# The last gate/up chunk of each expert as two loads of 1 MB with 8 KB pieces

## The reference

```python
logits = jnp.dot(x, w_router).astype(f32) + b_router.astype(f32)
top_val, top_idx = lax.top_k(logits, TOP_K)
gates = jax.nn.softmax(top_val, axis=-1)
...
def expert_block(args):
    xb, e = args
    gu = jnp.dot(xb, w_gate_up[e]) + b_gate_up[e]
    g = jnp.minimum(gu[:, :D_FF], SWIGLU_LIMIT)
    up = jnp.clip(gu[:, D_FF:], -SWIGLU_LIMIT, SWIGLU_LIMIT)
    hdn = (up + 1.0) * (g * jax.nn.sigmoid(SWIGLU_ALPHA * g))
    return jnp.dot(hdn, w_down[e]) + b_down[e]
```

## Time and profile before

| | before |
|---|---|
| median of three runs | 1271.97 us |
| the profiled execution | 1272.08 us |
| its span, first to last instruction | 1270.4 us |
| mean granted TensorE clock | 0.989 |
| PE busy | 1230.2 us (97%) |
| DVE / POOL / ACT busy | 465.4 / 242.9 / 174.7 us |
| read from HBM | 437.39 MB |
| DMA packets | 69352, of them 44744 under 8 KB |

### The profile page before, as it was taken

How to read it: one execution, slowest core, us unless ns; L and a number is a source line. 1 busy time by engine, 2 the same in 40 slices (tenths; PEclk the granted TensorE clock), 3 DMA queues, 4 the chain that set the end, 5 groups by cost and what they waited for, 6 DMA issues and landing times.

```text
span 1270.4 us, 21490 instructions
## 1 busy us (share of the span) xinstructions
PE 1230.2 (97%) x7739; PEld 553.7 (44%) x7740; DVE 465.4 (37%) x915; ACT 174.7 (14%) x311; POOL 242.9 (19%) x438
## 2 busy tenths in 40 slices
PE   7999999999899999999999999999999999999997
PEld 4666666668533333333334333333333333333332
DVE  6667767333522332222223222222223322222224
ACT  4651105214400000000000000000000000000002
POOL 2067760000211111111111211111111121111100
PEclk9989999999799999999999999999999999999999
DMA  8323232459699999999999999999999999999994
GB/s 227 99 68 100 87 105 75 155 184 385 231 393 428 428 427 428 429 427 429 429 428 429 429 429 428 428 428 429 429 428 429 429 428 429 428 429 427 428 429 187
DMA packets 69352, 440.31 MB, mean 347 GB/s; under 512 B 13024, under 2 KB 42376, under 8 KB 44744
## 3 DMA queue, kind: packets, MB, share of 16 engines
q1 hardware_dynamic: 66952, 438.72, 83.9%
q10 hardware_dynamic: 2368, 1.15, 0.3%
HBM read 437.39 MB, written 1.87 MB: 346 GB/s over the span
## 4 chain that ended last, share of the span: by engine, by line
PE 68%; DMA 25%; DVE 4%; issue 1%; SPq 0%; ACT 0%; DVEq 0%; POOL 0%; ACTq 0%; POOLq 0%
DMA big<-in_w_gate_up_dram 25%; PE psum L916 23%; PE psum L519 14%; PE psum L955 13%; PE psum L897 5%; PE psum L883 4%; PE psum L497 3%; PE psum L797 3%; PE psum L531 1%; PE psum L628 1%; PE psum L925 1%; PE psum L942 1%; DMA cst<-in_consts_dram 0%; PE psum L639 0%; DVE acc L1836 0%
## 5 line engine op out<-in xcount | busy, mean ns | idle before, releaser
L916 PE MATMUL psum<-big,m 128*64 128x512 f32 x2048 | 473.6, 599 | 13.0 <-DMA big<-in_w_gate_up_dram 10.0
L1797 DVE TENSOR_TENSOR acc<-acc,psum 128x512 f32<-128x512 f32 (+1 forms) x192 | 123.1, 681 | 583.4 <-PE psum L897 583.4
L916 PEld LDWEIGHTS psum<-big,m 128*64 128x64 f32 x2048 | 137.4, 137 | 320.0 <-issue 257.2
L955 PE MATMUL psum<-big,m 128*64 128x512 f32 x1024 | 226.8, 595 | 0.0
L519 PE MATMUL psum<-big,m 128*128 128x320 f32 x576 | 167.6, 447 | 3.2 <-issue 1.9
L1353 POOL COPY m<-uT 96x64 bf16 x32 | 7.5, 235 | 662.1 <-PE psum L942 661.7
L519 PEld LDWEIGHTS psum<-big,m 128*128 128x128 f32 x576 | 109.7, 195 | 55.1 <-issue 15.7
L955 PEld LDWEIGHTS psum<-big,m 128*64 128x64 f32 x1024 | 70.7, 137 | 134.1 <-issue 127.9
L897 PE MATMUL psum<-m 64*128 64x512 f32 (+1 forms) x384 | 106.7, 632 | 0.0
L1239 ACT ACTIVATE m<-m 128x512 f32<-128x512 f32 x32 | 20.2, 630 | 561.1 <-DVE m L1810 561.1
L1362 POOL TENSOR_SCALAR m<-cst,m 128x128 f32<-128x128 f32 x96 | 75.0, 792 | 7.7 <-POOL m L1357 7.7
(11 more groups left out here) (283 smaller groups left out, 851.2 us busy)
## 6 DMA issues: line engine op xcount, KB each, us to landing
big<-in_w_gate_up_dram SPq DMA_DIRECT2D x128, 2048.0 KB, 29.4
big<-in_w_down_dram SPq DMA_DIRECT2D x64, 2048.0 KB, 31.1
m<-in_w_in_dram SPq DMA_DIRECT2D x18, 1024.0 KB, 5.2
m<-in_w_s_glu_dram SPq DMA_DIRECT2D x8, 512.0 KB, 4.3
m<-in_w_out_dram SPq DMA_DIRECT2D x3, 1024.0 KB, 5.7
acc<-in_x_prompt_dram SPq DMA_DIRECT2D x4, 512.0 KB, 5.4
m<-in_w_ml_out_dram SPq DMA_DIRECT2D x2, 1024.0 KB, 5.0
big<-in_w_out_dram SPq DMA_DIRECT2D x1, 1024.0 KB, 7.6
```

Of the source, the lines that this page charges most:

```text
L916: mm = pe.matmul(psum[SLOT * hf:SLOT * hf + SLOT, GB + gu, :], xeT[:, GU_CHUNKS * k + c, :], big[:, base:base + 512], start=(c + k == 0), ...
L955: mm = pe.matmul(psum[SLOT * hf:SLOT * hf + SLOT, DB, :], hT[:, m, c, :], big[:, base:base + 512], start=False, stop=(c == DN_CHUNKS - 1 a ...
L1797: v.tensor_tensor(x, x, psum[0:n, CB + hf, :], ALU.add).then_inc(S("added"), 1)
```

## The change

`expert_chunk` issues the last gate/up chunk (`c` = 3) as two loads: the first takes the `k` = 0 half (one row of 8 KB for each partition, every other row of the matrix) and raises `w_landed` of the slot as before; the second takes the `k` = 1 half and raises a new semaphore, `w_half0` for even `r` and `w_half1` for odd `r`. PE waits for the new semaphore before the first `k` = 1 matmul of that chunk. Both destinations are the same places of the ring as before, the other five chunks are as before, and so is the count that frees slots.

```diff
@@ expert_chunk
             if c < GU_CHUNKS:
                 row = 2 * c * P
                 src = a["w_gate_up"][0, bass.ds(e, 1), row:row + 2 * P, :].rearrange("a (p k) n -> p (a k n)", k=2)
+                if c == GU_CHUNKS - 1:
+                    eng.dma_start(dst[:, 0:CHUNK], src[:, 0:CHUNK]).then_inc(S(f"w_landed{k}"), 16)
+                    eng.dma_start(dst[:, CHUNK:WIDE], src[:, CHUNK:WIDE]).then_inc(S(f"w_half{r % 2}"), 16)
+                    return
             else:
@@ expert, on PE
                     for c in range(GU_CHUNKS):
                         pe.wait_ge(S(f"w_landed{slot(r, c)}"), 16 * loads(turn_, r, c))
                         for k in range(2):
+                            if c == GU_CHUNKS - 1 and k == 1:
+                                pe.wait_ge(S(f"w_half{r % 2}"), 32 * turn_ + 16 * (r // 2 + 1))
                             for gu in range(2):
```

## The result

| | before | changed |
|---|---|---|
| median (lowest to highest) of 15 runs | 1271.84 us (1269.35 to 1273.61) | 1275.4 us (1272.98 to 1278.21) |
| profiled execution / its span | 1272.08 / 1270.4 us | 1275.22 / 1273.4 us |
| DMA packets | 69352 | 73969 |
| instruction blocks fetched (queue q8) | 21, 0.34 MB | 30, 0.49 MB |
| instructions of PE in the built program | 1842 | 1854 |

The change makes the kernel slower by 0.32% (ratio 1.0032, 95% interval 1.0024 to 1.0040); the medians are 3.6 us apart. 1273.8 was forecast, with a range of 1271.2 to 1277.0. The ratios in this document leave out every execution that took over 1.5% longer than the fastest of its kernel: two of e2's six and two of e10's seven.

The account below looks back on a forecast made before the run. The prediction took the unbroken DMA stream of weights (the belt), plus the last expert's work, to bound the kernel. Packets +2.0 us and earlier last start -0.24 us gave +1.8 us: 1273.8 us, range 1271.2 to 1277.0.

Parts of the forecast that it names:

- The belt bounds, and only what lengthens it counts: Weight stream, unbroken from about 380 us: added belt time is paid in full, PE time saved before the end is worth nothing.
- Term 1: Belt: the split adds 9 packets per engine and expert at 7.5 ns, 68 ns; 30 experts pay, +2.0 us.
- b: Price of a byte on one engine, 0.0368 ns, solved from 16 KB gate/up loads and 1 KB-piece w_in loads.
- the skipped-read rival: Split loads: reading every other 8 KB is slower, 0.48 us more per chunk, +14 us, 1286; chance 6%.
- Term 2: Last expert's fourth chunk: its first half lands earlier, so PE starts 0.24 us sooner, -0.24 us.
- Term 3: Other belt-paced experts: the same 0.24 us is given back waiting at the next expert's first chunk; worth nothing.
- it would be repaid out of the ring's stock: Stage paced by PE: a passed wait costing PE a few ns is made up from loaded chunks; no net cost.
- The first wait of PE about one expert earlier: Sign of being right: PE first waits for a load about one expert earlier, as the stock falls faster.
- faster, 7%: Whole kernel faster by over 0.2%: nearly all from the fourth-chunk wait being on the path, -3.0 us, rival's chance 8%.
- slower by over 0.2%: Whole kernel over 2.5 us slower: 35%, from dearer packets (24), load-end cost (5) and skipped reads (6).
- within 0.2%: Whole kernel within 2.5 us, not told from no change: 58%, including 13 for free extra packets.

Follow-up runs that it names:

- e2: Kernel before plus only a second, never-waiting wait before the fourth gate/up chunk's k = 1 matmuls, loads unchanged; median 1283.99 us, ratio 1.0062.
- e10: The change itself, unaltered, run again on the same chip as e11; 1277.49 us, ratio 1.0039 against the kernel before.
- e3: Kernel before with all four gate/up chunks as two 1 MB loads of 8 KB pieces, awaited once per chunk; 1285.86 us, ratio 1.0104.
- e5: Kernel before with all four gate/up chunks as single 2 MB loads, but of 8 KB pieces; 1280.79 us, ratio 1.0067.
- e11: The kernel of e8 run again, on the same chip as e10; 1273.78 us, ratio 1.0018 against the kernel before.
- e8: The change with two of PE's three signals per expert that nobody waits for left out; 1274.05 us, ratio 1.0021 against the kernel before.
- e7: Kernel before with gate/up chunks loaded in pairs, 4 MB loads of 32 KB pieces, and two unused signals per expert left out; 1274.00 us, ratio 1.0019.

## Why the prediction was right and where it was not

*The belt bounds, and only what lengthens it counts:* right where PE does not pause. The pace late in the loop is 29.44 us for the 29.43 forecast, at a DMA share of 1.01.

*Term 1, 68 ns per expert from nine packets of 7.5 ns:* right in size, and that by two errors that nearly cancel. Measured 74 ns ((1231.82 - 996.32) / 8 = 29.44 against 29.364), from eight pieces at 9.2 to 9.7 ns, a quarter dearer than forecast, and an end packet of about 1 ns where 7.5 was put. Over 30 experts that is +2.2 us, for 2.0. One row was misread on the way: the five full slices aren't within one load. With the slices beside them they add up to 2.1 MB, so they run over two w_in loads back to back; the sum stands as it is, since their seam belongs to the price. And that w_in pieces "fit the same b" is no argument against the skipped-read rival, since b was worked out from them; what removes it is e3 against e5.

*Term 2, -0.24 us at the end:* right (0.30 in the profile). *Term 3,* the same start given back at the next expert: right, 0.55 us of waiting for the 0.4 forecast.

*What failed* is the sentence in term 3 that if a wait cost PE anything, "it would be repaid out of the ring's stock". It priced the added instructions by the time they take, a few ns, and never asked what the code's length does where the loop jumps back. The pause is 6.7 us of PE. One of them, early, is mostly repaid from the stock, as the sentence says, but not wholly: places come free late, the loads issued from 470 to 490 us have only about 10 to 11 us from issue to landing where e11's have 18, so fewer are queued, and from 450 to 520 us the belt moves 29.4 MB where e8 and e11 move 29.9, about 1.2 us less. e8 and e11 put the change without pauses at +0.21% and +0.18%, close to the +0.14% forecast, and the change itself stands at +0.32% and +0.39%. That the pauses cost something is shown by e10 beside e11; how much is known only roughly, about 2 us there, and the single profiled executions say less (the last expert begins at 1231.82 us in the change's, at 1230.31 and 1231.59 in e8's and e11's). With seven pauses the stock is gone and the kernel takes 1303 us.

*Luck.* The result lies in the range, but the sum has no term for the pauses. The range held them because it had room for dearer packets and for the spread of the runs, and because none of the fifteen executions took as long as many pauses make it (the longest 1278.21 us, a little outside). Two of e10's seven, the same kernel, lie far above 1277.0.

*"The first wait of PE about one expert earlier"* was wrong for the same reason: it comes at 976.67 us (0.18 us, then 0.55 at 996.32) and not before 876.10, since PE was 6.7 us behind. Without the pause it comes true: e11's first wait is at 848.71, one expert earlier, and e8's at 827.92.

*The chances:* faster, 7%, is excluded by the interval. The result lies in the part given 35%, slower by over 0.2%; the forecast of a change within 0.2% holds for the change without the pauses only as far as its intervals (0.12 to 0.30% and 0.09 to 0.27%) reach.

## What to carry to other kernels

Where one queue is busy without a gap, a split that lets an engine start sooner buys only the last start, here 0.3 us, and pays for every piece in every round, here 9.4 ns each. Price added instructions in a written-out loop also by the loop's length: look in the timeline at the first instruction after each jump back, and in the instruction queue at the blocks fetched; eight instructions decided here between no pause and one to seven, of about 6.8 us each. Run such a kernel many times, because three runs can miss the bad case.

## What the runs showed of the hardware that I had not expected

- A jump back over a loop of PE that has grown by 9 to 14 instructions (whole program 1842 to between 1851 and 1856) can pause PE for 3.8 to 5.5 us and cost another 1.6 to 2.7 us while the granted clock is 0.50 at first; about 9 blocks of 16 KB are fetched for each. It happens at one to seven of seven jumps, for the same kernel at one (the change) or at seven (e10). Whether the kernel before ever pauses is not shown: its one profile has no pause, and its slowest execution took 1276.94 us.
- The price of a piece is 9.2 to 9.7 ns on its engine from 4 KB to 32 KB, and 32 KB pieces are not cut up (e7 moves its bytes in 9217 packets less than the kernel before); a load more costs about 1 ns.
- With two thirds of the bytes in loads that write 64 partitions each, the stream moves 214 to 221 GB/s at a DMA share of 1.01, half of the 428 GB/s that loads over 128 partitions move.
